# Two transformer blocks on one Trainium2 core: modulation chunks moved, convolution steps spread, two loops turned

## The chip, the cores and the metric

One of the eight cores of a Trainium2 chip runs the whole program. Its engines work side by side and each takes its own instructions in order: TensorE (PE; its weight loads are shown as PEld), VectorE (DVE), ScalarE (ACT), GpSimd (POOL) and SyncE (SP), which issues loads. They wait for one another by semaphores. The metric is the device time of one execution in microseconds (us), the median of several runs.

## The reference, cut to what matters

Two layers of a first block, then one layer of a second, on 256 tokens of width 1024, all in float32:

```python
for l in range(2):                                    # the first layers
    h = rms_norm(x, norm_mix_pre[l]); proj = h @ w_in[l]
    # a: compressed, selected and windowed attention; d: windowed attention with sinks
    # b: c = a * sigmoid(gate); causal depthwise convolution, 31 taps; layer_norm; silu
    # c: pooling over 2, 4, 8, 16 tokens, minus the input, times a matrix
    up = einsum("bsnc,ncd->bsnd", branches, w_branch[l])
    gates = sigmoid(h @ w_gate[l])
    mix = sum_n(gates * up) @ w_o[l]
    x = x + rms_norm(mix, norm_mix_post[l])
    hf = rms_norm(x, norm_ffn_pre[l])
    u = causal_depthwise_conv(hf @ ffn_w_up[l], ffn_conv_w[l], ffn_conv_b[l])
    f = (gelu(gate(u)) * val(u)) @ ffn_w_down[l]
    x = x + rms_norm(f, norm_ffn_post[l])
# second block: it is modulated by silu(c) @ w_mod + b_mod and silu(c_ctx) @ w_mod + b_mod (6 x 1024 values
# each), then state space scan, attention, mixture of experts
```

The modulation depends on `c` and `c_ctx` alone, not on `x`, so its product can be computed at any time before the second block.

## The kernel before, in words

**Chunks and the ring.** All weights stream from HBM in chunks of 1 MB (128 x 2048 floats) through a ring of four slots. A first layer has 92 chunks, so layer 1 starts in slot 0 again. Chunk c lies in slot c % 4. SP (`sync_program`, line 445, its load is line 450) takes the slots in turn: it waits until the slot's chunk is released (`used`), then issues the load of the chunk four places later, which reports to `landed`. PE releases a chunk with its last matmul (`done_with`) or, after `release`, with the first matmul of what it does next (`carry`).

**Split chunks.** Most products are made of three passes of a faster format. ACT copies a landed chunk to a rounded high part (`split_hi`, line 415, instruction at 423), DVE subtracts it from the chunk for the low part (`split_lo`, line 425, instruction at 428, written to `ring_low` at the same slot), and PE multiplies high by high, high by low and low by high. The high parts have buffers of their own, two up to the output product, so chunk n's high part waits until PE is through with chunk n - 2; in the FFN stage there are four. Both splits stand at fixed places in ACT's and DVE's programs. "Raw" chunks (modulation, compression) are multiplied as they land.

**Order of the chunks in a layer.** Input projections (kv, kv2, q, dq, two chunks each; 24 matmuls a chunk), c, ba, bg with the compression between, 16 gate chunks, 8 branch ("up") chunks, 4 of the output product `w_o` (wo), 22 of the FFN, 11 of down. Modulation: a layer computes half of its 6 x 1024 columns x 2 in 6 steps of 512 columns, each of two raw chunks, or halves (`mod_half`, line 487, matmuls at 495, four of them on 32 output rows each), copied by ACT (`mod_out`), summed and turned by PE (`mod_turn`, line 503, 508), and added up by DVE (`mod_in`). Before, halves stand behind gate chunks 2, 3, 5, 6, 8, 9 and FFN chunks 1, 3, 6, 8, 11, 13.

**Rounds.** Attention runs in six rounds beside the gate chunks, two gate chunks a round (PE's loop: `scores`, a gate chunk, `turn_probs`, a gate chunk, `values`). DVE's round r: `mask` of both halves (1299), the split of gate chunk 2r + 1, `out_low`, `weigh` (1326), the split of 2r + 2, 12 convolution steps (`conv_steps`, 1255; a step is one of 31 taps on one of 4 channel blocks, 124 in all, line 1267). In round 1 the weighing of the compressed attention (`cmp_weigh`, 1345) follows the split. PE transposes its result (`cpT`) behind gate chunk 2. Two more stretches of 8 and 6 steps follow the rounds.

**Branches.** PE makes 16 products `up`, four for each branch in the order pooling, a, d, b (`BRANCH_ORDER` = 2, 0, 3, 1). DVE multiplies each by its gate, POOL adds them up. Between them DVE does the steps that are left (3, 5, 3, 5, then all). PE transposes the finished convolution before product (0, 3) (`CONV_BEFORE`, `conv_turns`), DVE normalises it (`conv_norm`, POOL takes the root), PE transposes it back before (3, 1) and (3, 2) (`OB_BEFORE`), ACT applies silu, and DVE's low parts of it (`ob_lo`) are needed by branch b. 

**Output product and down.** Both go over column halves c outermost; for each of wo's chunks, or of down's, both token tiles t of 128 are multiplied. When (c, t) is complete ACT squares it (`post_square`, line 1083), and when both halves of a tile have squares, POOL takes the root, DVE adds the normalised tile to x (`residual`, 1467), ACT squares x (887), POOL takes the root, ACT (892) and DVE (1146) scale, and PE transposes the tile (`turn_normed`, 482). The order of the splits around it is written out, for ACT in these lines; DVE's (1472) are alike:

```python
for c in range(2):                                        # line 1085
    for n in range(FIRST_WO + 2 + 2 * c, FIRST_WO + 4 + 2 * c):
        split_hi(act, n)          # c = 0: wo 2, 3; c = 1: FFN 0, 1
    for t in range(TT):
        post_square("wo", c, t)
```

At the end of layer 0 ACT and DVE do the next layer's splits 0 and 1 (`heads`: `highs`, `lows`, lines 437 to 443, called at 1124 and 1510) ahead of the squares and the residual of down's c = 1. Between layer 1 and block 2 all engines meet at a barrier.

**PSUM regions.** `plan_layer` (line 215) fixes the region of every product; `claim` waits until the one before it in that region is drained.

Of the kernel before, what the change touches and what calls it, by code (L numbers as in the profile page):

```python
# [214 lines left out]
def plan_layer(jobs):  # L215
    for t in range(TT):
        for c in range(2):
            jobs.plan(("ht", t, c))
# [40 lines left out]
    for i in range(MOD_STEPS // 2):  # L259
# [18 lines left out]
    for i, r in zip(range(3, MOD_STEPS), ("s0", "s1", "t")):  # L278
# [7 lines left out]
CONV_BEFORE = (0, 3)  # L286
OB_BEFORE = {(3, 1): 0, (3, 2): 1}
# [3 lines left out]
def layer_block(nc, l, mem, ring, ring_low, landed, used, wts, psum, sems, cols_dram, rows_dram, turner_in, placed, wait_x, wait_scratch):  # L291
# [161 lines left out]
    def tensor_program(pe):  # L453
# [32 lines left out]

        def mod_half(i, half):
# [28 lines left out]
        def next_split():  # L516

            n = split_at["n"]
            split_at["n"] += 1
            assert state["chunk"] == SPLIT_CHUNKS[n], (state, n)  # L520
# [11 lines left out]
        pe.wait_ge(turner_in, 16)  # L532
        turn_normed("ht", 1)

        for w in ("kv", "kv2", "q", "dq"):
            for half in range(2):
# [19 lines left out]
                else:  # L556
                    jobs.fill(mm, (w, 1))
                    release(w)

# [242 lines left out]
        for c in range(2):  # L802
            for half in range(2):
                hi, lo = (part.rearrange("p (k n) -> p k n", k=4) for part in next_split())
                for i in range(2):
                    pe.wait_ge(mix_lo, 2 * half + i + 1)
                for t in range(TT):
                    name, ts = ("wo", c, t), slice(t * P, (t + 1) * P)
                    if half == 0:
                        jobs.claim(pe, name)  # L810
                    for k in range(4):
                        kk = 4 * half + k
                        mm = pe.matmul(jobs.out(name), mixS[:, 0, kk, ts], hi[:, k, :], start=(kk == 0), stop=False)
                        if k == 0:
                            carry(mm)
                        pe.matmul(jobs.out(name), mixS[:, 0, kk, ts], lo[:, k, :], start=False, stop=False)
                        mm = pe.matmul(jobs.out(name), mixS[:, 1, kk, ts], hi[:, k, :], start=False, stop=(kk == KD - 1))
                    if half == 1:
                        jobs.fill(mm, name)
                if half == 0:  # L820
                    done_with(mm)
                else:
                    release(("wo", c, 1))

        turn_normed("hf", 2)
# [20 lines left out]
        for i in range(FB // 2):  # L846
            hi, lo = (part.rearrange("p (q n) -> p q n", q=BLOCKS) for part in next_split())
            for t in range(TT):
                ts = slice(t * P, (t + 1) * P)
                for q in range(BLOCKS):  # L850
                    c, n = divmod(BLOCKS * i + q, FB)
                    name = ("down", c, t)
                    if n == 0:
                        jobs.claim(pe, name)
                    if c == 0 and t == 0:
                        pe.wait_ge(f_ready, n + 1)
# [2303 lines left out]
```

## Time and profile before

| | us |
|---|---|
| median of 3 runs (1822.49 to 1829.71) | 1823.33 |
| the profiled execution's own time | 1830.08 |
| its span, first to last instruction | 1828.0 |
| PE busy | 1680.5 |
| DVE busy | 1084.7 |
| ACT busy | 760.2 |
| POOL busy | 261.6 |

The mean granted clock of TensorE is 0.951 of 2.4 GHz. Layer 0 fills the span's first 548 us, layer 1 ends at about 1090, the rest is block 2. The span is 2 us shorter than the execution's own time. In a row of a profile L482 is line 482 of the kernel, `out<-in` are the program's names, and `<-` in brackets or behind a bar names who ended the idle time before an instruction.

### The profile page before, as it was taken

How to read it: one execution, taken by the hardware profiler on the slowest of the kernel's cores; microseconds unless marked ns; L12 is line 12 of the kernel's file. 1: busy time of each engine (PE TensorE's matmuls, PEld its weight loads, DVE VectorE, ACT ScalarE, POOL GpSimd, SP SyncE). 2: the span in 40 equal slices, each digit the busy share in tenths (PEclk: the TensorE clock that was granted, in tenths of full speed). 3: DMA queues.
4: the chain of work that ended last, by engine and by line, in shares of the span. 5: the costliest groups of instructions: out<-in, count | busy, mean ns of one | idle time of the engine just before them, and what ended most of it. 6: DMA issues, size and time to landing. Idle time of an engine off the chain costs nothing. (4 is left out here: it accounts for less than half of the span.)

```text
span 1828.0 us, 26603 instructions
## 1 busy us (share of the span) xinstructions
PE 1680.5 (92%) x10712; PEld 1383.9 (76%) x10712; DVE 1084.7 (59%) x1490; ACT 760.2 (42%) x1069; POOL 261.6 (14%) x293
## 2 busy tenths in 40 slices
PE   7998997899998989998899989999898978999996
PEld 5887897699977888887799974445475537899995
DVE  4668987566645668987566631284547334454555
ACT  4355654455534355554455422113116224333431
POOL 0200004144301200003144200014320000000000
PEclk9999998899999999998899999999869987999998
DMA  6544454466553545454466554112000232355551
GB/s 252 185 185 162 185 185 151 149 234 250 184 200 139 211 157 184 169 178 158 151 237 224 187 185 170 69 69 91 25 23 1 70 115 93 139 184 184 184 182 70
DMA packets 40121, 282.07 MB, mean 154 GB/s; under 512 B 4816, under 2 KB 5072, under 8 KB 6864
## 3 DMA queue, kind: packets, MB, share of 16 engines
q1 hardware_dynamic: 38432, 273.15, 41.4%
q10 hardware_dynamic: 1584, 7.42, 1.2%
q8 instruction: 78, 1.28, 0.3%
q14 instruction: 27, 0.22, 0.0%
HBM read 279.50 MB, written 1.05 MB: 153 GB/s over the span
## 5 line engine op out<-in xcount | busy, mean ns | idle before, releaser
L428 DVE TENSOR_TENSOR ring_low<-ring,sb_hi 128x2048 fp32r<-128x2048 f32 x116 | 267.9, 2309 | 192.3 <-ACT sb_hi L423 191.9
L423 ACT ACTIVATE sb_hi<-ring 128x2048 fp32r<-128x2048 f32 x116 | 222.5, 1918 | 285.9 <-DMA ring<-weights 114.4
L577 PE MATMUL psum<-sb_hS,sb_hi 128*128 128x256 f32 x704 | 203.3, 289 | 4.8 <-DVE ring_low L428 4.7
L1848 DVE TENSOR_TENSOR sb_split<-ring,sb_split 128x2048 fp32r<-128x2048 f32 x48 | 109.9, 2292 | 153.2 <-ACT sb_split L1843 153.2
L580 PE MATMUL psum<-sb_hS,sb_hi 128*128 128x256 f32 x704 | 200.3, 284 | 0.0
L581 PE MATMUL psum<-sb_hS,ring_low 128*128 128x256 f32 x704 | 199.4, 283 | 0.0
L839 PE MATMUL psum<-sb_hfT,ring_low 128*128 128x256 f32 x704 | 198.1, 281 | 0.0
L2162 PE MATMUL psum<-sb_hfS,sb_split 128*128 128x256 f32 x512 | 146.5, 286 | 6.0 <-DVE sb_hfS L2692 3.9
L2165 PE MATMUL psum<-sb_hfS,sb_split 128*128 128x256 f32 x512 | 145.8, 285 | 0.0
L2166 PE MATMUL psum<-sb_hfS,sb_split 128*128 128x256 f32 x512 | 145.8, 285 | 0.0
L577 PEld LDWEIGHTS psum<-sb_hS,sb_hi 128*128 128x128 f32 x704 | 134.9, 192 | 14.1 <-DVE ring_low L428 7.2
L581 PEld LDWEIGHTS psum<-sb_hS,ring_low 128*128 128x128 f32 x704 | 136.3, 194 | 0.0
L580 PEld LDWEIGHTS psum<-sb_hS,sb_hi 128*128 128x128 f32 x704 | 134.7, 191 | 0.0
L839 PEld LDWEIGHTS psum<-sb_hfT,ring_low 128*128 128x128 f32 x704 | 134.5, 191 | 0.0
L428 DVE TENSOR_TENSOR ring_low<-ring,sb_hi_ffn 128x2048 fp32r<-128x2048 f32 x34 | 79.7, 2350 | 64.2 <-ACT sb_hi_ffn L423 64.2
L1843 ACT ACTIVATE sb_split<-ring 128x2048 fp32r<-128x2048 f32 x48 | 91.4, 1906 | 54.2 <-PE psum L2130 18.1
L835 PE MATMUL psum<-sb_hfT,sb_hi_ffn 128*128 128x256 f32 x384 | 109.9, 286 | 1.3 <-DVE sb_hfT L1153 1.3
L838 PE MATMUL psum<-sb_hfT,sb_hi_ffn 128*128 128x256 f32 x384 | 109.7, 286 | 0.0
L2162 PEld LDWEIGHTS psum<-sb_hfS,sb_split 128*128 128x128 f32 x512 | 99.3, 194 | 8.3 <-issue 8.0
L1267 DVE SCALAR_TENSOR_TENSOR sb_acc<-sb_bglu,sb_cols,sb_acc 128x256 f32<-128x256 f32 x240 | 101.5, 495 | 0.0
L2165 PEld LDWEIGHTS psum<-sb_hfS,sb_split 128*128 128x128 f32 x512 | 99.3, 194 | 0.3
L2166 PEld LDWEIGHTS psum<-sb_hfS,sb_split 128*128 128x128 f32 x512 | 99.2, 194 | 0.0
(392 smaller groups left out, 3881.7 us busy)
## 6 DMA issues: line engine op xcount, KB each, us to landing
ring<-weights SPq DMA_DIRECT2D x256, 1024.0 KB, 4.8
sb_rows_ffn<-rows ACTq DMA_DIRECT2D x4, 512.0 KB, 4.7
sb_rows_mix<-rows ACTq DMA_DIRECT2D x2, 1024.0 KB, 5.0
sb_rows<-rows ACTq DMA_DIRECT2D x1, 2048.0 KB, 9.1
sb_x<-x_in SPq DMA_DIRECT2D x2, 512.0 KB, 5.9
sb_y<-ctx_in SPq DMA_DIRECT2D x1, 1024.0 KB, 6.4
out<-sb_x SPq DMA_DIRECT2D x2, 512.0 KB, 2.7
sb_const<-const SPq DMA_DIRECT2D x1, 711.0 KB, 13.5
```

Source lines behind the costliest of these rows:

```text
L423: act.activation(hi_of(n), ring[:, c % SLOTS, :], ACT.Copy).then_inc(hi_ready, 1)
L428: eng.tensor_tensor(low_of(n), ring[:, SPLIT_CHUNKS[n] % SLOTS, :], hi_of(n).bitcast(F32), ALU.subtract).then_inc(lo_dve, 1)
L577: mm = pe.matmul(out, hi[:, k, bs], hS[:, 0, k, :], start=(k == 0), stop=False)
L580: pe.matmul(out, hi[:, k, bs], hS[:, 1, k, :], start=False, stop=False)
L581: mm = pe.matmul(out, lo[:, k, bs], hS[:, 0, k, :], start=False, stop=(k == KD - 1))
L835: mm = pe.matmul(out, hi[:, k, b * P:(b + 1) * P], hfT[:, 0, k, :], start=(k == 0), stop=False)
L838: pe.matmul(out, hi[:, k, b * P:(b + 1) * P], hfT[:, 1, k, :], start=False, stop=False)
L839: mm = pe.matmul(out, lo[:, k, b * P:(b + 1) * P], hfT[:, 0, k, :], start=False, stop=(k == KD - 1))
L1848: dve.tensor_tensor(split[:, n % SPLITS, 1, :], ring[:, (first_moe + n) % SLOTS, :], split[:, n % SPLITS, 0, :].bitcast(F32), ALU.subtract ...
L2162: mm = pe.matmul(out, hi[:, k, b * P:(b + 1) * P], hfS[:, 0, k, :], start=(k == 0), stop=False)
L2165: pe.matmul(out, hi[:, k, b * P:(b + 1) * P], hfS[:, 1, k, :], start=False, stop=False)
L2166: mm = pe.matmul(out, lo[:, k, b * P:(b + 1) * P], hfS[:, 0, k, :], start=False, stop=(k == KD - 1))
```

## The change

Six halves a layer move. Two (step 0) now stand between the two chunks of kv, and PE does them at the layer's head: in layer 1 before it transposes the normalised tiles, in layer 0 behind. Four (steps 3 and 4) stand between wo's last chunk and the FFN's first. The other six are behind gate chunks 2, 3, 6, 7 and FFN chunks 11, 13. PSUM regions, `mod_out`, `mod_turn` and `mod_in` follow them. Convolution steps are given per round, 102 in place of 84; all that are left come behind the first product; its transposes move from product (0, 3) to (2, 3), those of the branch from (3, 1), (3, 2) to (0, 2), (3, 0). `cmp_weigh` goes ahead of a split. The last two chunks of wo and of down are multiplied tile by tile: both chunks for t = 0, then both for t = 1. No matmul is added or removed; the placing of the splits around wo's squares and of the next layer's first splits is not changed. The diff, cut:

```diff
-MOD_AFTER_GATE = {2: (0, 0), 3: (0, 1), 5: (1, 0), 6: (1, 1), 8: (2, 0), 9: (2, 1)}
-TURN_AFTER_GATE = {4: 0, 7: 1, 10: 2}
-MOD_AFTER_FFN = {1: (3, 0), 3: (3, 1), 6: (4, 0), 8: (4, 1), 11: (5, 0), 13: (5, 1)}
-TURN_AFTER_FFN = {5: 3, 10: 4, 15: 5}
+HEAD_MODS = [(0, 0), (0, 1)]
+MOD_AFTER_GATE = {2: (1, 0), 3: (1, 1), 6: (2, 0), 7: (2, 1)}
+TURN_AFTER_GATE = {4: 1, 8: 2}
+MODS_AFTER_WO = [(3, 0), (3, 1), (4, 0), (4, 1)]
+MOD_AFTER_FFN = {11: (5, 0), 13: (5, 1)}
+MOD_OUT_IN_FFN = {1: 3, 3: 4, 14: 5}
+TURN_AFTER_FFN = {3: 3, 7: 4, 15: 5}
...
-    return ["split"] * FIRST_BA + ["raw", "split"] * 4 + gates + ["split"] * 12 + ffn + ["split"] * (FB // 2)
+    return (["split"] + ["raw"] * len(HEAD_MODS) + ["split"] * (FIRST_BA - 1) + ["raw", "split"] * 4 + gates + ["split"] * 12
+            + ["raw"] * len(MODS_AFTER_WO) + ffn + ["split"] * (FB // 2))
...
-CONV_BEFORE = (0, 3)
-OB_BEFORE = {(3, 1): 0, (3, 2): 1}
+CONV_BEFORE = (2, 3)
+OB_BEFORE = {(0, 2): 0, (3, 0): 1}
+CONV_STEPS = (4, 20, 16, 14, 16, 14, 18)
...
+        def head_mods():
+            if wait_down is not None:
+                wait_down(pe)
+            for i, half in HEAD_MODS:
+                state["chunk"] = 1 + half
+                mod_half(i, half)
+            state["chunk"] = 0
...
         pe.wait_ge(turner_in, 16)
+        if l > 0:
+            head_mods()
         turn_normed("ht", 1)
+        if l == 0:
+            head_mods()
...
+            if w == "kv":
+                mod_turn(0)
...
+        last = []
+        for t in range(TT):
             for half in range(2):
...
+                if t == 0:
+                    last.append([part.rearrange("p (k n) -> p k n", k=4) for part in next_split()])
+                mm = mix_product(1, half, t, *last[half])
+                if (t, half) == (1, 0):
+                    mm.then_inc(used[(state["chunk"] - 2) % SLOTS], 1)
+        release(("wo", 1, 1))
+
+        for i, half in MODS_AFTER_WO:
+            mod_half(i, half)
         turn_normed("hf", 2)
...
-        for n in range(FIRST_UP + 2, FIRST_UP + 6):
+        for n in range(FIRST_UP + 2, FIRST_UP + 4):
             split_hi(act, n)
         for t in range(TT):
-            if t == 1:
-                split_hi(act, FIRST_UP + 6)
+            split_hi(act, FIRST_UP + 4 + t)
             jobs.wait_filled(act, ("obT", t))
...
+            if r == 1:
+                cmp_weigh()
             split_lo(dve, FIRST_GATE + 2 * r + 1)
...
-            if r == 1:
-                cmp_weigh()
...
-            conv_steps(12)
+            conv_steps(CONV_STEPS[r])
...
                 if i % 2 == 0:
-                    conv_steps(3)
+                    conv_steps(4 * TAPS)
                 else:
                     chunk = 2 * bi + i // 2
...
                     if chunk < 7:
                         split_lo(dve, FIRST_UP + chunk + 2)
-                    conv_steps(5 if chunk < 2 else 4 * TAPS)
...
+        conv_roots()
         k = 0
         for n in BRANCH_ORDER[1:]:
...
-                if (n, i + 1) == CONV_BEFORE:
-                    conv_roots()
...
+    kv0 = k_split(kv[:, 0:512])
     chunks = [
-        k_split(kv[:, 0:512]), k_split(np.concatenate([kv[:, 512:768], w[:, 1816:2072]], 1)),
+        kv0[0:1], *[mod[j][half] for j, half in HEAD_MODS], kv0[1:2], k_split(np.concatenate([kv[:, 512:768], w[:, 1816:2072]], 1)),
...
-        k_split(i["w_o"][l][:, 0:512]), k_split(i["w_o"][l][:, 512:1024]), *ffn,
+        k_split(i["w_o"][l][:, 0:512]), k_split(i["w_o"][l][:, 512:1024]),
+        *[mod[j][half] for j, half in MODS_AFTER_WO], *ffn,
```

Down's last two chunks are turned like wo's.

## Rows read from the trace of the kernel before

**Rows 1.** The page: PE's busy time and the granted clock in 40 slices.

```profile
PE 1680.5 (92%) x10712; PEld 1383.9 (76%) x10712; DVE 1084.7 (59%) x1490; ACT 760.2 (42%) x1069; POOL 261.6 (14%) x293
...
PEclk9999998899999999998899999999869987999998
```

**Rows 2.** Waits of PE up to 556 us: us in total, times, longest.

```profile
PE psum L482 <- ACT sb_tm L892: 25.6, 3, 11.4
...
PE psum L482 <- DVE sb_acc L1267: 8.2, 1, 8.2
...
PE psum L794 <- issue: 1.3, 1, 1.3
```

**Rows 3.** Groups of PE, whole run: modulation halves and turns; busy us, mean ns.

```profile
L495 PE MATMUL psum<-ring,sb_cvec 128*32 128x512 f32 x192 | 25.6, 605 | 0.0
...
L508 PE MATMUL psum<-sb_const,sb_mrow 128*128 128x2 f32 x96 | 11.4, 240 | 0.0
```

**Rows 4.** Stretches: us, busy PE, PEld, DVE, ACT, POOL, clock, DMA share, GB/s.

```profile
8.30:18.20 9.90, 5.72 (x21) 4.99 (x22) 6.88 (x8) 7.86 (x9) 2.30 (x4) 1.00 1.01 424
...
286.70:293.90 7.20, 7.20 (x52) 7.20 (x51) 4.24 (x8) 2.63 (x2) 3.05 (x6) 0.80 0.18 49
...
344.20:354.40 10.20, 7.25 (x33) 6.88 (x34) 5.25 (x7) 4.24 (x7) 2.25 (x3) 0.50 0.58 206
```

**Rows 5.** DVE in time order, rounds 0 and 1: start us, us, what.

```profile
134.16 3.25 DVE L1267 SCALAR_TENSOR_TENSOR sb_acc<-sb_bglu,sb_cols,sb_acc 128x256 f32<-128x256 f32 x8
...
139.96 2.28 DVE L428 TENSOR_TENSOR ring_low<-ring,sb_hi 128x2048 fp32r<-128x2048 f32 x1
...
149.50 4.83 DVE L1267 SCALAR_TENSOR_TENSOR sb_acc<-sb_bglu,sb_cols,sb_acc 128x256 f32<-128x256 f32 x12
```

**Rows 6.** The same kind of stretch, DVE alone, rounds 2 to 5: busy us.

```profile
158.04:221.35 63.31, 57.81 (x94) 1.00 0.53 196
```

**Rows 7.** PE in time order, single rows where the stages begin.

```profile
29.14 0.40 PE L547 MATMUL psum<-sb_hi,sb_hS 128*128 128x512 f32 x1
...
144.34 0.48 PE L482 MATMUL psum<-sb_const,sb_csc 128*128 128x128 f32 x1 [6.03 <-DVE sb_csc L1357]
...
221.41 0.39 PE L577 MATMUL psum<-sb_hS,sb_hi 128*128 128x256 f32 x1 [0.32 <-DVE ring_low L428]
...
346.50 0.47 PE L482 MATMUL psum<-sb_const,sb_tm 128*128 128x128 f32 x1 [6.62 <-ACT sb_tm L892]
...
555.48 0.45 PE L482 MATMUL psum<-sb_const,sb_tm 128*128 128x128 f32 x1 [7.54 <-ACT sb_tm L892]
```

**Rows 8.** ACT in time order around the output product of layer 0.

```profile
329.06 1.92 ACT L423 ACTIVATE sb_hi<-ring 128x2048 fp32r<-128x2048 f32 x1 [5.10 <-PE psum L813]
...
332.01 3.97 ACT L423 ACTIVATE sb_hi_ffn<-ring 128x2048 fp32r<-128x2048 f32 x2
...
337.15 0.60 ACT L1083 ACTIVATE sb_acc<-psum 128x512 f32<-128x512 f32 x1 [1.17 <-PE psum L817]
...
339.92 0.60 ACT L1083 ACTIVATE sb_acc<-psum 128x512 f32<-128x512 f32 x1 [2.08 <-PE psum L817]
```

**Rows 9.** DVE in time order, the same stretch.

```profile
331.01 2.29 DVE L428 TENSOR_TENSOR ring_low<-ring,sb_hi 128x2048 fp32r<-128x2048 f32 x1 [4.66 <-ACT sb_hi L423]
...
340.00 1.28 DVE L1467 SCALAR_TENSOR_TENSOR sb_x<-sb_tm,sb_small,sb_x 128x1024 f32<-128x1024 f32 x1 [0.50 <-POOL sb_small L1533]
```

**Rows 10.** SP in time order: the load of gate chunk 4.

```profile
138.48 0.33 SPq L450 DMA_DIRECT2D ring<-weights  x1
```

**Rows 11.** Loads of the ring issued from 316 to 335 us (four).

```profile
DMA to landing us min/median/max: 4.8/4.8/4.9
```

**Rows 12.** ACT and DVE in time order at the end of layer 0.

```profile
543.82 1.92 ACT L423 ACTIVATE sb_hi<-ring 128x2048 fp32r<-128x2048 f32 x1 [0.98 <-DMA ring<-weights]
...
547.98 0.60 ACT L1083 ACTIVATE sb_acc<-psum 128x512 f32<-128x512 f32 x1 [1.66 <-PE psum L861]
...
549.16 1.28 DVE L1467 SCALAR_TENSOR_TENSOR sb_x<-sb_tm,sb_small,sb_x 128x1024 f32<-128x1024 f32 x1 [0.50 <-POOL sb_small L1533]
```

More of the change, by code:

```diff
@@ L258, in plan_layer @@
             jobs.plan(("O", a, t), "u", drains=2)
-    for i in range(MOD_STEPS // 2):
+    for i in range(1, MOD_STEPS // 2):
         jobs.plan(("mod", i), "t")
@@ L277, in plan_layer @@
         jobs.plan(("ffn", j))
-    for i, r in zip(range(3, MOD_STEPS), ("s0", "s1", "t")):
+    for i, r in zip(range(3, MOD_STEPS), ("s0", "t", "s1")):
         jobs.plan(("mod", i), r)
@@ L800, in tensor_program, with mix_product @@
                 release(name)
-        for c in range(2):
-            for half in range(2):
[L804 to L823, printed above, removed]
+        def mix_product(c, half, t, hi, lo):
+            name, ts = ("wo", c, t), slice(t * P, (t + 1) * P)
+            if half == 0:
+                jobs.claim(pe, name)
+            for k in range(4):
+                kk = 4 * half + k
+                mm = pe.matmul(jobs.out(name), mixS[:, 0, kk, ts], hi[:, k, :], start=(kk == 0), stop=False)
+                if k == 0:
+                    carry(mm)
+                pe.matmul(jobs.out(name), mixS[:, 0, kk, ts], lo[:, k, :], start=False, stop=False)
+                mm = pe.matmul(jobs.out(name), mixS[:, 1, kk, ts], hi[:, k, :], start=False, stop=(kk == KD - 1))
+            if half == 1:
+                jobs.fill(mm, name)
+            return mm
@@ new lines, in tensor_program @@
+        for half in range(2):
+            hi, lo = (part.rearrange("p (k n) -> p k n", k=4) for part in next_split())
+            for i in range(2):
+                pe.wait_ge(mix_lo, 2 * half + i + 1)
+            for t in range(TT):
+                mm = mix_product(0, half, t, hi, lo)
+            if half == 0:
+                done_with(mm)
+            else:
+                release(("wo", 0, 1))
+        last = []
+        for t in range(TT):
+            for half in range(2):
+                if t == 0:
[3 more added lines that the diff above has]
+                    mm.then_inc(used[(state["chunk"] - 2) % SLOTS], 1)
@@ L847, in tensor_program @@
+        for i in range(FB // 2 - 2):
             hi, lo = (part.rearrange("p (q n) -> p q n", q=BLOCKS) for part in next_split())
             for t in range(TT):
[L849 to L856, printed above, removed]
[L857 to L863 removed]
@@ L864, in tensor_program @@
-            if i < FB // 2 - 1 and n < FB - 1:
+                mm, n = down_product(i, t, hi, lo)
+            if n < FB - 1:
                 done_with(mm)
             else:
-                release(name)
+                release(("down", 0, 1))
+        last = []
+        for t in range(TT):
+            for i in range(2):
+                if t == 0:
+                    last.append([part.rearrange("p (q n) -> p q n", q=BLOCKS) for part in next_split()])
+                mm, n = down_product(FB // 2 - 2 + i, t, *last[i])
+                if (t, i) == (1, 0):
+                    mm.then_inc(used[(state["chunk"] - 2) % SLOTS], 1)
@@ L868, in tensor_program @@
+        release(("down", 1, 1))
         jobs.wait_filled(pe, ("down", 1, 1))
```

59 lines of the change are left out of this document (39 added, 20 removed).

## The prediction

> **What bounds the kernel now.** I read the page first: the first two sections. TensorE (PE) is busy for 92% of the span, at a granted clock of 0.951 on average, that is 2.4 GHz nearly everywhere [rows 1]. So nothing that merely moves PE's work gains anything; only PE's idle stretches, and the stretches at the lower clock level behind them, can be won. Second, PE's waits. Up to 556 us (all of layer 0 and the head of layer 1) the three waits for the normalised tile come to 25.6 us, of which 11.4 is the start of the run; the convolution holds PE for 8.2 us, the branch parts for 1.3 [rows 2], the compressed weights for 6.03 [rows 7]. Layer 1 repeats them to within 0.2 us. The change aims at all of these. Third, the granted clock behind a wait: 0.50 from 344.2 to 354.4 us, 0.80 over 286.7 to 293.9 [rows 4]. The latter is 20% of 7.2 us = 1.4 us lost, and some 1 us more in the transposes ahead of it, 2.4 in all. Last, the order of instructions on ScalarE (ACT) and VectorE (DVE) around each idle stretch, which decides this case.
>
> **Modulation halves.** A half is 25.6 us / 24 = 1.07 us busy [rows 3], some 1.0 us of displacement as its end overlaps the next matmul. A turn is 11.4 / 12 = 0.95 us. Moving them is worth at most that: a layer has 12 halves, 6 of them now in the FFN stage, of which 4 leave: -4.0 us there. The other cost is where their chunks stand in the ring of 4 slots. A load is issued only when the chunk four places earlier is released, and it lands 4.8 us later [rows 11]. Splitting it takes 1.9 us on ACT and 2.3 on DVE [rows 8, 9]. Backlogged loads come faster: 424 GB/s at the start [rows 4], 2.5 us per 1 MB chunk. I use 4.8 us after the issue or 2.5 us after the landing before, whichever is later.
>
> **Head of a layer.** The order is now kv0, two halves, kv1, kv2. The load of kv2's first chunk waits for kv0's release, so it is ready for PE 4.8 + 0.2 + 1.9 + 2.4 = 9.3 us later; PE has only kv1 (24 matmuls, 5.6 us, twice the 2.8 us between the two squares [rows 8]) and a turn of 0.95. It waits 2.8 to 2.9 us. In layer 0 the halves add some 1.3 us before kv0's release, since one wait of 1.1 us hides part. So kv2, which began at 29.14 [rows 7], begins 1.3 + 0.95 + 2.9 = **5.2 us later**.
>
> In layer 1 the halves lie in the gap before 555.48. But the splits of the next layer's first two chunks are issued by ACT and DVE ahead of the squares and the residual of down's second half. The second split is ring chunk 3 now, not 1, and its slot is that of down's very last chunk, released when down is complete. Before, it began at 543.82, and the last square, which marks down's end, at 547.98 [rows 12]. After: the load is issued 0.2 us behind that, landed 553.0, split by ACT 555.0, squares only then, DVE's low part until 557.3, post_gain 0.7, the residual of tile 0 from 557.95 instead of 549.16 [rows 12]: **8.8 us later**, and PE's transposes with it (they follow its end by 5.0 us, before and after). Then the same kv2 delay, 0.95 + 2.9 or 3.0. Together 12.7.
>
> **Rounds.** Convolution steps take 4.83 / 12 = 0.40 us [rows 5]. Round 0 has 4 instead of 12 and the weighing precedes a split. DVE's order then: the first 4 steps end at 134.16, mask 2.7 (from the end of the next 8 steps, 137.3, to the split at 139.96), weigh the compressed part 2.1 (from the split's end, 142.2, to 144.3, when PE's wait of 6.03 ends [rows 7]), split 2.3, so that wait shrinks to below 1 and gate chunk 3 starts 5 us earlier. But then DVE runs late: it weighs round 1 (143.4), waits for the high part of gate chunk 4 (issued at 138.48 [rows 10], landed at 143.3 in either kernel, 1.9 on ACT), splits until 147.5, and does 20 steps, until 155.5. Round 2's mask begins at 155.5, 2.5 us before the old 158.04, and some 4 us after its scores are there. From 158.04 to 221.35 DVE was busy 57.8 of 63.3 us [rows 6]. 10 more steps in rounds 2 to 4 are 4.0 us, against 5.5 idle, of which an estimated 4 (waits for scores and for a load) can go. So that stretch lasts about 63 us again, and gate chunk 11, at 221.41 [rows 7], starts **2.5 us earlier**, though two halves and a turn (3 us) have left the rounds before it: DVE has become the bound. Bounds: 0, if ACT's exps slip too, and 6.5, if DVE had room. I take 2.5, since the row of busy time is the nearer. The cover that is used up is DVE's slack: 86% busy before.
>
> **Convolution.** 116 steps are done before the branch products instead of 98. The last 8 (3.2 us) end after the first product, PE's transposes three products in then find them done. The wait of 8.24, the 1.29 for the branch parts and 2.4 of lower clock go. What is late next is the split of up chunk 3: ACT may start it only when chunk 1's buffer is free, DVE does conv_norm (3.6 us) first: 1.0 us. **10.9 earlier**. GpSimd's roots go ahead of its additions, and wait for nothing that those need.
>
> **Output product, tile outermost.** Its last chunk is needed 2.8 us earlier, but its high part shares a buffer with the second one and starts only at 329.06, released by PE [rows 8]; the low part ends at 333.30 [rows 9]. PE wants it at 331.3: 2.0 us of wait. Tile 0 is complete 0.9 us earlier, tile 1 and the stage 2.0 later. Down has four buffers, its last chunk is split long before; no cost, and no gain as tile 1 still comes last and the barrier follows.
>
> **The gap before the FFN.** This is the largest term. ACT issues the splits of FFN chunks 0 and 1 between the squares of the two column halves: the 3.97 us at 332.01, then the squares at 337.15 and 339.92 [rows 8]. DVE likewise, ahead of the residual. With four halves in between, FFN chunk 0 has the slot of half 0, and half 0 is read only after the output product ends. Step by step on the clock of before: product ends 341.8; half 2 lands 344.1 (its slot is freed at 339.2), half 3 at 347.5, FFN chunk 0 at 350.0, chunk 1 at 352.5. ACT splits until 354.4, the squares start there and not at 337.15; the low part of chunk 1 ends at 356.7; the residual of tile 0 runs 357.4 to 358.7 (before: 340.00 to 341.28, [rows 9]), and the transposes follow 5.2 us later as they did: 363.9 against 346.50 [rows 7], **17.4 us later**, the 2.0 included. The four halves (4.0) are hidden there. The lower clock (10.2 us at 0.50 around 346.5 [rows 4]) is not saved: PE is idle for 15 us.
>
> The DMA page of the Trainium skill (DMA: Bandwidth & Descriptors, Bandwidth) puts HBM at some 358 GB/s per core. By it chunks would land 2.9 us apart, and each of these gaps would be 1 to 2 us longer, the total 3 us more. The measured 424 GB/s decides here.
>
> **Sum.** Layer 0: 5.2 - 2.5 - 10.9 + 17.4 - 4.0 = +5.2. Layer 1: 12.7 - 2.5 - 10.9 + 17.4 - 4.0 = +12.7. Block 2 is untouched. Total +17.9: span 1828.0 to 1845.9. The profiled execution took 1830.08, 6.8 above the median of 1823.33 and 0.4 above the slowest run; against the median this is **1841**.
>
> **Rivals.** *Chunks arrive in time, faster.* If the FFN chunks and kv1 were there before the squares, nothing would hold them: transposes would follow half 3, 2.0 us later than before, at the head 0. Layer 0: 5.2 - 2.5 - 10.9 + 2.0 - 4.0 = -10.2; layer 1: 3.9 - 2.5 - 10.9 + 2.0 - 4.0 = -11.5; 1801.6. It takes delays of squares (15.4 + 15.4 + 8.8 = 39.6) below some 22 to be not slower. For: loads overlap, and some of the lower clock would be won too. Against: four slots and in-order engines leave no way. *Rounds have slack.* DVE keeps up and the 6.5 us of the cpT wait come through: 8 less, 1833; the idle 5.5 of 63.3 us speak against it. *Rounds stall.* Each round gets later and ACT's exps and splits add to it: gate chunk 11 no earlier, and 2 us more in the up stage: 1850. *Little moves (within 0.5%).* Slot releases and splits overlap better by half (delays 8, 8, 4 instead of 15.4, 15.4, 8.8): 1822. *The change doesn't do what it says* for the last two down chunks: their order buys nothing, 0 us, within all cases.
>
> **Chances.** Forecast 0.58 (own range 1834 to 1850). Rounds with slack 0.09, rounds stalling 0.10, little moves 0.14, faster 0.09. A measurement of this kernel tells about 0.5% (9 us) from no change. Slower by more than that: 0.58 + 0.09 + 0.10 = 0.77, same 0.14, faster 0.09. The range of 8 in 10 goes from 1823, the upper part of the little-moves case, to 1855, stalled rounds with some longer stretches of the lower clock on top.
>
> **What would show it.** After the output product, ACT's idle before the split of FFN chunk 0, ended by the DMA, and squares 12 us or more behind PE's last matmul. PE's wait ahead of the FFN transposes near 15 us instead of 6.62, at layer 1's head near 13 instead of 7.54. A wait of some 3 us for the low part of kv2, of 2 for the last output chunk. No wait for the convolution. Waits of PE for low parts in the rounds, 1 to 3 us in each of rounds 2, 3 and 5. Squares that come at once behind the product would make all of it wrong; so would loads that land while the product still runs.

## The result and the profile after

The changed kernel takes 1855.18 us (median of 4, 1848.67 to 1857.83) against 1826.52 us of the kernel before: ratio 1.0151, 95% interval 1.0112 to 1.0191. Slower, as forecast, but at the far end: 1841 was the value, 1834 to 1850 its own range, and the median lies 0.2 us past the wide range (1823 to 1855). Run again beside 11 executions of the kernel before: 1852.27 against 1828.60 us, 1.0140 (1.0119 to 1.0161). The loss is 24 to 29 us.

The profiled execution, the quickest of its four, took 1848.67 us with a span of 1846.7 us. That is 18.7 us above the profiled span of before (1828.0), where 17.9 was forecast. The difference to the 24 to 29 us is spread: the profiled execution of before (1830.08) was near the upper end of that kernel's executions (1818.7 to 1831.0 in 61 of them), the one of after at the lower end of its own.

The page of the changed kernel [rows 1]:

```profile
PE 1676.5 (91%) x10712; PEld 1375.5 (74%) x10712; DVE 1084.4 (59%) x1490; ACT 760.3 (41%) x1069; POOL 243.7 (13%) x293
```

PE does the same work in 4 us less, and the span is longer: everything lost is idle time. Waits of PE up to 566 us (shortly before the end of layer 1's head gap), changed kernel [rows 2]; us in total, times, longest:

```profile
PE psum L489 <- ACT sb_tm L945: 25.9, 2, 14.5
PE psum L601 <- DVE ring_low L435: 10.1, 6, 2.6
PE psum L511 <- DMA ring<-weights: 4.1, 3, 2.7
PE psum L833 <- DVE ring_low L435: 2.8, 2, 1.8
PE psum L524 <- ACT sb_mrow L954: 1.9, 1, 1.9
```

The 8.2 us for the convolution are gone, and of the 6.0 for the compressed weights 0.7 are left. The 25.9 us for the normalised tile are two waits, not three, the third (13.22 us) ends at 568.12, outside this stretch. New are waits for the low parts of gate chunks in the rounds (L601, 10.1 us against 2.4 before), for the halves' loads, for the last output chunk, for the copy of the modulation row.

Layer 0 by stage, as five stretches that begin with PE's instruction: the head's transposes, the transpose of the compressed part (rounds), the branch products, the output product, the FFN's transposes (to the next layer's). Columns as in [rows 4]. Kernel before:

```profile
11.40:144.30 132.90, 122.14 (x862) 105.99 (x862) 83.89 (x123) 62.83 (x96) 11.05 (x17) 0.99 0.53 195
144.30:256.80 112.50, 111.18 (x879) 97.25 (x879) 95.06 (x159) 66.10 (x118) 0.00 (x0) 0.98 0.49 178
256.80:316.20 59.40, 49.80 (x400) 49.22 (x401) 48.37 (x65) 22.82 (x22) 16.80 (x14) 0.91 0.45 160
316.20:346.50 30.30, 22.70 (x96) 17.89 (x96) 20.89 (x17) 16.63 (x20) 9.23 (x12) 0.96 0.40 139
346.50:555.50 209.00, 200.80 (x1409) 182.90 (x1409) 123.50 (x137) 101.27 (x120) 64.43 (x77) 0.97 0.58 210
```

Changed kernel, and behind the five the two stretches of low clock around the long gaps:

```profile
11.30:143.00 131.70, 124.75 (x887) 106.99 (x887) 78.81 (x115) 63.17 (x97) 11.05 (x17) 0.99 0.55 205
143.00:260.10 117.10, 107.75 (x855) 94.84 (x855) 106.99 (x185) 66.21 (x118) 0.00 (x0) 0.99 0.44 162
260.10:308.10 48.00, 47.46 (x400) 47.05 (x400) 40.72 (x47) 22.93 (x22) 14.67 (x14) 1.00 0.54 198
308.10:356.50 48.40, 27.90 (x129) 18.61 (x129) 21.09 (x17) 16.48 (x20) 10.16 (x12) 0.82 0.45 174
356.50:568.10 211.60, 196.20 (x1392) 180.51 (x1392) 124.39 (x137) 101.03 (x120) 56.15 (x77) 0.97 0.52 188
338.90:359.40 20.50, 4.84 (x22) 3.10 (x23) 12.34 (x11) 9.66 (x14) 7.72 (x10) 0.50 0.53 201
557.40:571.10 13.70, 2.98 (x14) 2.98 (x15) 10.12 (x10) 6.99 (x13) 7.75 (x10) 0.50 0.00 0
```

The branch stage falls from 59.4 to 48.0 us and has PE busy 47.5 of it: the gain that was meant. The output product with what follows it grows from 30.3 to 48.4 with 5.2 us more of work (the 4 halves). The rounds grow by 4.6 us although PE has 3.4 us less to do; DVE's work there rises from 95 to 107 us. PE's rows where it waits in the rounds, the last of them at gate chunk 11:

```profile
165.45 0.58 PE L601 MATMUL psum<-sb_hS,sb_hi 128*128 128x256 f32 x1 [2.60 <-DVE ring_low L435]
...
204.24 0.39 PE L601 MATMUL psum<-sb_hS,sb_hi 128*128 128x256 f32 x1 [2.30 <-DVE ring_low L435]
...
224.71 0.39 PE L601 MATMUL psum<-sb_hS,sb_hi 128*128 128x256 f32 x1 [2.26 <-DVE ring_low L435]
```

The order of events at the long gap in layer 0 [rows 7, 8, 9]: single rows of PE, then ACT, DVE.

```profile
325.27 0.50 PE L833 MATMUL psum<-sb_hi,sb_mixS 128*128 128x512 f32 x1 [1.79 <-DVE ring_low L435]
...
333.53 0.40 PE L837 MATMUL psum<-sb_hi,sb_mixS 128*128 128x512 f32 x1
...
340.02 1.93 PE L511 MATMUL psum<-ring,sb_cvec 128*32 128x512 f32 x8 [2.72 <-DMA ring<-weights]
356.50 0.90 PE L489 MATMUL psum<-sb_const,sb_tm 128*128 128x128 f32 x3 [14.54 <-ACT sb_tm L945]
...
342.47 1.91 ACT L430 ACTIVATE sb_hi_ffn<-ring 128x2048 fp32r<-128x2048 f32 x1 [18.44 <-DMA ring<-weights]
344.94 1.91 ACT L430 ACTIVATE sb_hi_ffn<-ring 128x2048 fp32r<-128x2048 f32 x1 [0.57 <-DMA ring<-weights]
346.76 0.58 ACT L1137 ACTIVATE sb_acc<-psum 128x512 f32<-128x512 f32 x1
...
350.27 1.28 DVE L1521 SCALAR_TENSOR_TENSOR sb_x<-sb_tm,sb_small,sb_x 128x1024 f32<-128x1024 f32 x1 [0.49 <-POOL sb_small L1587]
```

The product ends at 333.9. ACT is idle for 18.44 us in front of the split of FFN chunk 0, ended by the DMA, and the first square starts 12.9 us behind the product's end, behind two such splits. It is the square of tile 0, which in the turned order was complete at about 328.3, 5.6 us ahead of the product's end. PE, with the halves done at 341.95, waits 14.54 us. At layer 1's head ACT does the same for kv's second chunk:

```profile
556.57 1.91 ACT L430 ACTIVATE sb_hi<-ring 128x2048 fp32r<-128x2048 f32 x1 [11.90 <-DMA ring<-weights]
558.38 0.58 ACT L1137 ACTIVATE sb_acc<-psum 128x512 f32<-128x512 f32 x1
```

### The profile page after: what moved, and what is told of

It is laid out like the page before. It is cut to its first block and busy times, and to the rows that moved or that the text cites. A ratio compares the mean times of both kernels' runs of the same rounds, so it can differ in the third digit from the quotient of the medians.

```text
span 1846.7 us, 26597 instructions
## 1 busy us (share of the span) xinstructions
PE 1676.5 (91%) x10712; PEld 1375.5 (74%) x10712; DVE 1084.4 (59%) x1490; ACT 760.3 (41%) x1069; POOL 243.7 (13%) x293
## 5 line engine op out<-in xcount | busy, mean ns | idle before, releaser
L601 PE MATMUL psum<-sb_hS,sb_hi 128*128 128x256 f32 x704 | 203.7, 289 | 20.2 <-DVE ring_low L435 20.1
L601 PEld LDWEIGHTS psum<-sb_hS,sb_hi 128*128 128x128 f32 x704 | 135.1, 192 | 30.9 <-DVE ring_low L435 24.0
L1896 ACT ACTIVATE sb_split<-ring 128x2048 fp32r<-128x2048 f32 x48 | 91.4, 1906 | 54.2 <-PE psum L2183 18.1
L430 ACT ACTIVATE sb_hi_ffn<-ring 128x2048 fp32r<-128x2048 f32 x34 | 65.2, 1918 | 82.4 <-DMA ring<-weights 75.2
```

The lines of the kernel that those rows point to most:

```text
L430: act.activation(hi_of(n), ring[:, c % SLOTS, :], ACT.Copy).then_inc(hi_ready, 1)
L601: mm = pe.matmul(out, hi[:, k, bs], hS[:, 0, k, :], start=(k == 0), stop=False)
```

## The experiments

Theory: three things that the change carries along cost what it loses, namely splits that wait for late chunks ahead of the squares (FFN chunks 0 and 1; kv's second chunk), and convolution steps ahead of the gate chunks' low parts. Rivals: the halves themselves, the turned orders, the clock. Each median stands against the kernel before in the same session (1827.6 to 1828.9 us), 11 to 18 executions of it. Medians of different sessions are compared directly below; the kernel before differed by 1.3 us between them.

**1. The convolution part alone, on the kernel before.**

```diff
-CONV_BEFORE = (0, 3)
-OB_BEFORE = {(3, 1): 0, (3, 2): 1}
+CONV_BEFORE = (2, 3)
+OB_BEFORE = {(0, 2): 0, (3, 0): 1}
+CONV_STEPS = (4, 20, 16, 14, 16, 14, 18)
...
-            conv_steps(12)
+            conv_steps(CONV_STEPS[r])
...
```

> The kernel before with the convolution part of the change alone (steps spread over the rounds, its normalisation and transposes moved to the third branch, ACT's and DVE's splits of the up chunks placed accordingly); no half and no chunk order is touched. Theory (the loss is all in the halves' new places, the convolution part is a pure gain): the wait of 11 us for the convolution goes, wo starts 10 to 13 us earlier in each layer, the time is 20 to 26 us below the kernel before, about 1803 us. Rival (the spread steps make VectorE the bound of the rounds, and it is the halves that left the rounds that pay for it): the gates stage gets 3 to 6 us longer in each layer and the gain is 10 to 14 us, about 1814 us.

1809.50 us, ratio 0.9900 (0.9878 to 0.9923), 19 us below the kernel before. Between theory and rival: its rounds and its branch stage are

```profile
138.40:257.20 118.80, 111.83 (x879) 97.36 (x879) 107.14 (x186) 66.37 (x119) 0.00 (x0) 0.97 0.49 178
...
257.20:305.20 48.00, 47.48 (x400) 47.08 (x400) 40.73 (x47) 22.93 (x22) 14.69 (x14) 1.00 0.55 198
```

So the branch stage gives 11.4 us a layer and the head some 6 (the wait of 6.03), and the rounds take 6.3 of it back: 118.8 against 112.5 us with the same work of PE. This part alone beats both kernels. The rounds grew as the rival said, and here no half has left them.

**2. The same, with the steps distributed otherwise.**

```diff
-CONV_STEPS = (4, 20, 16, 14, 16, 14, 18)
+CONV_STEPS = (4, 13, 18, 14, 11, 18, 22)
```

> The convolution part alone with other numbers of steps in the rounds (4, 13, 18, 14, 11, 18, 22 instead of 4, 20, 16, 14, 16, 14, 18). Theory (in the changed rounds VectorE's steps stand ahead of the low parts of the gate chunks, 0.4 us each, and these are what TensorE waits for): the waits of 2.7 and 2.0 us in rounds 2 and 5 go, 3 to 4.5 us less in each layer, about 1802 us. Rival (the waits come from ACT's splits or from the DMA and only move): within 2 us of the run with 20 and 16, about 1809 us.

1795.54 us, ratio 0.9824 (0.9804 to 0.9844): 14 us less than with the first distribution, more than the 7 expected. Rounds of layer 0, and PE's waits in the rounds, first of this kernel:

```profile
137.30:250.10 112.80, 109.75 (x879) 94.95 (x879) 106.23 (x184) 65.80 (x119) 0.00 (x0) 1.00 0.51 187
```

```profile
PE psum L578 <- DVE ring_low L429: 2.2, 3, 0.9
```

and of the one with 20 and 16 steps:

```profile
PE psum L578 <- DVE ring_low L429: 5.6, 3, 2.7
```

With the smaller waits of the stretch 7.7 us of waiting have become 3.7. 4.0 us of waits have gone and 6.0 us of time: the granted clock of the stretch is 1.00 instead of 0.97, and PE's busy time for the same 879 matmuls falls by 2.1 us. These 2.1 us belong to one of the two long waits: behind the wait of 2.75 us (it ends at 161.01) the clock was 0.72 over 10 us, behind the one of 1.98 us (221.82) it was 1.00. DVE's rounds hold 100 steps instead of 102; the two others are done behind the first branch product, where the stage grows from 48.0 to 49.6 us. Both layers' rounds together give 11.8 of the 14 us.

**3. FFN chunks 0 and 1 split behind the normalisation.**

```diff
 for c in range(2):
-    for n in range(FIRST_WO + 2 + 2 * c, FIRST_WO + 4 + 2 * c):
-        split_hi(act, n)
+    if c == 0:
+        for n in range(FIRST_WO + 2, FIRST_WO + 4):
+            split_hi(act, n)
     for t in range(TT):
         post_square("wo", c, t)
 squares_of(1)
 norm_first(1)
+for n in range(FIRST_FFN, FIRST_FFN + 2):
+    split_hi(act, n)
```

(DVE's low parts alike, behind `norm_second`.)

> The changed kernel, with the splits of FFN chunks 0 and 1 (ACT's and DVE's) moved from ahead of the squares of the output product's second half to behind the normalisation's last instruction on each engine. Theory (these splits wait for chunks whose slots are freed late, and the squares stand behind them): the squares start right behind the product, 10 to 12 us earlier, the wait of 14.5 us ahead of the FFN's transposes falls to 2 to 5 us in both layers, the time falls by 18 to 24 us to about 1834 us. Rival (the halves on TensorE themselves, and not the splits, set the start of the FFN): the transposes can't start before the halves end, the gain is under 6 us in all, about 1850 us.

1835.85 us, ratio 1.0051 (1.0031 to 1.0071): 16 to 19 us below the changed kernel, at the lower edge of the 18 to 24 expected. ACT and PE at the gap (the trace is of an execution of 1843.86 us, the slowest of seven):

```profile
339.46 0.60 ACT L1137 ACTIVATE sb_acc<-psum 128x512 f32<-128x512 f32 x1 [5.26 <-PE psum L837]
...
347.83 1.91 ACT L430 ACTIVATE sb_hi_ffn<-ring 128x2048 fp32r<-128x2048 f32 x1 [2.70 <-DMA ring<-weights]
...
347.23 3.68 PE L489 MATMUL psum<-sb_const,sb_tm 128*128 128x128 f32 x16
...
356.78 0.55 PE L874 MATMUL psum<-sb_hfT,sb_hi_ffn 128*128 128x256 f32 x1 [5.87 <-DVE sb_hfT L1210]
```

The squares are now released by PE's product and nothing else; the transposes follow the halves with no wait. A new wait of 5.87 us stands behind them: the late splits now delay the high and low parts of the normalised tile. The cost of such a split moves with it, wherever something urgent stands behind it.

**4. The halves between product and FFN put back.**

```diff
-MODS_AFTER_WO = [(3, 0), (3, 1), (4, 0), (4, 1)]
-MOD_AFTER_FFN = {11: (5, 0), 13: (5, 1)}
+MODS_AFTER_WO = []
+MOD_AFTER_FFN = {1: (3, 0), 3: (3, 1), 6: (4, 0), 8: (4, 1), 11: (5, 0), 13: (5, 1)}
...
```

> The changed kernel with the four halves between the output product and the FFN put back among the FFN's blocks, where they stood before (head, rounds, convolution and tile orders stay changed). Theory: FFN chunks 0 and 1 land some 10 us earlier again and the wait ahead of the FFN's transposes is 6 to 8 us as in the kernel before; 20 to 22 us between product and transposes become 7, the FFN gets 6 us longer, 8 to 10 us gained in each layer, about 1837 us. Rival (the turned tile order of the output product is what delays the FFN's chunks, since it frees the slots later): the wait stays over 10 us and the gain is under 6 us in all, about 1850 us.

1830.51 us, ratio 1.0016 (1.0001 to 1.0030): 22 to 25 us less, more than the 18 expected. The FFN chunks' splits run inside the product again, and PE's wait is

```profile
326.07 3.85 ACT L430 ACTIVATE sb_hi_ffn<-ring 128x2048 fp32r<-128x2048 f32 x2
...
343.35 0.90 PE L489 MATMUL psum<-sb_const,sb_tm 128*128 128x128 f32 x3 [5.76 <-ACT sb_tm L945]
```

The turned order is still in this kernel, so it is not what delays the chunks. This is the largest single loss of the change.

**5. kv's second chunk ahead of the halves in the ring.**

```diff
-                state["chunk"] = 1 + half
+                state["chunk"] = 2 + half
...
-        kv0[0:1], *[mod[j][half] for j, half in HEAD_MODS], kv0[1:2], k_split(np.concatenate([kv[:, 512:768], w[:, 1816:2072]], 1)),
+        kv0[0:1], kv0[1:2], *[mod[j][half] for j, half in HEAD_MODS], k_split(np.concatenate([kv[:, 512:768], w[:, 1816:2072]], 1)),
```

> The changed kernel with the first two halves put behind kv's second chunk in the order of the ring (chunks 2 and 3 instead of 1 and 2), so that kv's second chunk no longer waits for the slot of the last down chunk; TensorE's order is unchanged. Theory: at the second layer's head the squares no longer stand behind that split, the wait ahead of the transposes falls from 13.2 to 4 to 6 us, the time falls by 7 to 10 us to about 1846 us; the first layer's head stays. Rival (the squares wait for something else, the drains of the down product or the two halves on TensorE): under 2 us, about 1854 us.

1846.80 us, ratio 1.0112 (1.0090 to 1.0133): 5.5 to 8.4 us less, where 7 to 10 were expected. The split is out of the way of the second square, which PE releases; the first, of tile 0, still stands behind it:

```profile
552.99 1.92 ACT L430 ACTIVATE sb_hi<-ring 128x2048 fp32r<-128x2048 f32 x1 [2.62 <-DMA ring<-weights]
554.81 0.58 ACT L1137 ACTIVATE sb_acc<-psum 128x512 f32<-128x512 f32 x1
...
557.26 0.60 ACT L1137 ACTIVATE sb_acc<-psum 128x512 f32<-128x512 f32 x1 [1.78 <-PE psum L899]
```

PE's wait ahead of the transposes is gone, where 4 to 6 us were expected to stay; in its place PE waits 2.33 and 1.11 us for the loads of the two halves and begins the transposes right behind them, at 564.56. From the FFN's transposes of layer 0 to those of layer 1's head the trace has 202.3 us instead of 211.6, 9.3 less. But layer 0's head got 6.9 us longer (138.6 against 131.7; below, run 9), so the gain in time is what is left of the two.

**6. Both repairs (4 and 5) together.**

> The changed kernel with both repairs: the four halves back among the FFN's blocks, and the first two halves behind kv's second chunk in the ring. Theory (the two losses are at different places and add): the changed kernel's 1853 us less 24 and less 8, about 1822 us; this is 10 us above the run that has the same convolution part and the same turned orders but no half moved (1811.7 us), and these 10 us stand in the two heads and the rounds (TensorE's wait of 2 us for the turned rows' copy, kv2's chunks a place later, three waits instead of two in the rounds, each with a stretch of half clock behind it). Rival (one repair makes the other void, or the chunks collide again): over 1828 us.

1823.84 us (13 executions, 1820.27 to 1835.55), ratio 0.9984 (0.9969 to 0.9998). They add up: 29.5 us less than the changed kernel (1853.3), where the two alone gave 22.8 and 6.5.

**7. The turned orders alone, on the convolution part.** Both loops over the last two chunks as in the changed kernel, no half moved.

> The kernel before with the convolution part and the turned tile orders of the output and down products (no half is moved). Theory (a turned order finishes token tile 0 some 2.8 us sooner ahead of the end of the product, but TensorE waits 1.8 us for the product's last split): the wait of 6.5 us ahead of the FFN's transposes becomes 4 us and one of about 2 us stands in the product; 1 us or less a place, the time within 3 us of the run with the convolution part alone, about 1808 us. Rival (the turned order is a gain that the halves' damage hid): 2.5 us at each of four places, about 1800 us. Second rival (the first of the last chunks is freed late and costs more than that): about 1813 us.

1811.65 us, ratio 0.9915 (0.9894 to 0.9935), 2 us above run 1 and not to be told from it. In its trace the FFN's wait is 5.76 us instead of 6.52, and a wait of 1.8 us for the last split stands in the product: the stage takes 31.5 us against 30.4, in layer 1 33.1 against 30.3. The turn gains nothing.

**8. The output product's order put back in the changed kernel.**

```diff
-        for t in range(TT):
-            for half in range(2):
...
-                mm = mix_product(1, half, t, *last[half])
...
+        for half in range(2):
...
+            for t in range(TT):
+                mm = mix_product(1, half, t, hi, lo)
...
```

> The changed kernel with the output product's last two chunks in their old order (both token tiles of a chunk, then the next chunk). Theory (the halves' chunks and the splits behind them set the start of the FFN, not this order): TensorE's wait of 1.8 us for the last split goes, the halves' chunks have their slot freed 3 us sooner; 1 to 4 us less a layer, about 1850 us. Rival (the turned order is what lets the squares start early, and it is lost): 2 to 3 us more a layer, about 1860 us.

1848.06 us, ratio 1.0111 (1.0091 to 1.0131), 4 us less than the changed kernel in the same session (1852.27). The wait of 1.8 us goes, and the stage takes 46.4 us instead of 48.3; the gap stays, since the DMA sets it:

```profile
339.02 1.06 PE L511 MATMUL psum<-ring,sb_cvec 128*32 128x512 f32 x8 [3.37 <-DMA ring<-weights]
355.52 0.69 PE L489 MATMUL psum<-sb_const,sb_tm 128*128 128x128 f32 x2 [15.43 <-ACT sb_tm L944]
```

**9. Both repairs, old orders, the steps of run 2.** It differs from run 2 only by the two halves in each head and the places of the others in the rounds.

> The changed kernel with both repairs, both tile orders back and the other numbers of steps (4, 13, 18, 14, 11, 18, 22), so that it differs from the run with these numbers and no half moved (1795.5 us) only by two halves in each head and by the places of the four in the rounds. Theory (a half in TensorE's gap at the head is cheap in itself, but kv2's chunks come later and TensorE waits for the turn's row, some 3 us a head with the clock behind it; in the rounds two halves less are worth as much as their 1.5 us each): 4 to 8 us above it, about 1801 us. Rival (halves in the gaps are the gain they are meant to be once nothing stands behind them): 3 to 6 us below it, about 1791 us.

1813.92 us, ratio 0.9922 (0.9904 to 0.9939): 18 us above run 2, where 4 to 8 were expected; the sign was right, the size wrong. Layer 0's head and rounds:

```profile
11.70:150.50 138.80, 128.94 (x887) 108.38 (x887) 78.72 (x115) 63.07 (x97) 11.03 (x17) 0.99 0.51 194
...
150.50:262.60 112.10, 106.91 (x855) 93.66 (x855) 106.28 (x183) 65.91 (x118) 0.00 (x0) 1.00 0.46 170
```

and the head of run 2:

```profile
11.60:137.30 125.70, 120.28 (x863) 104.75 (x863) 78.66 (x114) 62.61 (x96) 11.04 (x17) 1.00 0.52 197
```

In the rounds the two halves that left give 0.7 us for 2.8 us of work; in the head they cost 13.1 (layer 1: 7.7, from the starts of the stages, 133.4 against 125.7). PE's rows say why:

```profile
18.60 1.94 PE L511 MATMUL psum<-ring,sb_cvec 128*32 128x512 f32 x8 [0.56 <-DMA ring<-weights]
...
35.62 1.02 PE L524 MATMUL psum<-sb_const,sb_mrow 128*128 128x2 f32 x8 [2.07 <-ACT sb_mrow L944]
37.45 0.50 PE L569 MATMUL psum<-sb_hi,sb_hS 128*128 128x512 f32 x1 [0.80 <-DVE ring_low L435]
```

A half takes 1.94 us here and not 1.07, as PE runs at half its pace this early (kv's matmuls too, until 24 us; run 2 was at full pace from 16.4, which makes some 3.6 of the 13.1 us); then come the turn (1.02), 2.07 us for the copy of the row and 0.80 for kv2, 3.9 us together. kv2 starts 9.8 us later; the other 3.3 us come behind it, where the granted clock is 0.80 up to 46 us and PE waits another 1.08 us for a low part. In run 2 kv2 starts at about 27.6 (its matmuls run on without a wait from 16.37, 48 of them), here at 37.45. In layer 0 there is no gap to put a half in. In layer 1 there is one, and the stage with the gap takes as long as in run 2 (207.3 against 207.2 us); what is lost there is lost behind it, where PE waits 1.97 us for the copy of the row and 0.62 for kv2 and then has 0.58 of the clock for 7 us.

**10. The changed kernel with the steps of run 2.** `CONV_STEPS` as in run 2, no other edit.

> The changed kernel with the other numbers of steps in the rounds (4, 13, 18, 14, 11, 18, 22) as its one edit. Theory (two of the three waits of TensorE in its rounds come from the steps standing ahead of the gate chunks' low parts, whatever became of the halves, and a stretch of half clock follows each): the rounds get 4 to 6 us shorter in each layer, 8 to 14 us in all, about 1842 us. Rival (with two halves fewer in the rounds the waits come from elsewhere): under 4 us, about 1850 us.

1850.24 us, ratio 1.0138 (1.0113 to 1.0163): 2 to 5 us less than the changed kernel by the medians and nothing by the ratios (1.0140 there), where 8 to 14 were expected. The rounds did what was expected; here they are, then the output stage and the FFN of layer 0,

```profile
145.90:257.70 111.80, 106.73 (x855) 93.66 (x855) 106.24 (x183) 65.98 (x118) 0.00 (x0) 1.00 0.47 170
306.60:356.40 49.80, 28.53 (x129) 19.68 (x129) 21.03 (x17) 16.49 (x20) 10.20 (x12) 0.82 0.44 170
356.40:570.30 213.90, 198.74 (x1392) 182.89 (x1392) 124.73 (x137) 101.21 (x120) 58.15 (x77) 0.95 0.52 185
```

and the same of the changed kernel run again:

```profile
145.50:261.50 116.00, 106.63 (x854) 93.58 (x854) 107.01 (x185) 66.27 (x118) 0.00 (x0) 1.00 0.46 164
309.50:357.80 48.30, 27.91 (x129) 18.62 (x129) 21.08 (x17) 16.48 (x20) 10.18 (x12) 0.82 0.47 175
357.80:569.40 211.60, 196.24 (x1392) 180.56 (x1392) 124.55 (x137) 101.08 (x120) 56.45 (x77) 0.97 0.53 187
```

4.2 us are won in the rounds (6.5 in layer 1), all of it waits: PE is busy for the same 106.7 us at a clock of 1.00 in both, though one of the waits that went was of 2.74 us. And 3.8 are given back in these two stages behind: PE is busy 2.5 us longer in the FFN for the same 1392 matmuls, at 0.95 of the clock instead of 0.97. Why the clock came back later there is not shown; the gap ahead is the same length (16.5 us from the start of the fourth half to the transposes in both).

**11. The changed kernel again.**

> The changed kernel again, to have its time and the granted clock of its executions beside many of the kernel before on one chip. Theory (the profiled execution of the changed kernel, 1848.7 us, was a quick one of its spread, and the one of before, 1830.1 us, a slow one): median 1853 to 1857 us against 1828 to 1829 us, and executions that differ by some 8 us do so by their mean granted clock (0.943 against 0.947) and not by a wait. Rival (the quick and the slow executions differ in a DMA's landing): the same clock, other waits.

1852.27 us (1850.11 to 1856.49), ratio as given at the top. The median is 0.7 us below the range expected. The quickest execution has the highest mean granted clock (0.946 at 1850.11) and the slowest the lowest (0.943 at 1856.49), but in between the order isn't kept: 1852.27 has 0.943 and 1853.32 has 0.945. Their waits are not known, as only the profiled one left a trace; that the clock is the cause, and not a companion, is not shown.

## Why the prediction was right, and where it was off

Medians of neighbouring kernels make a chain: before 1828.9; convolution part 1809.5 (-19.4); turned orders 1811.7 (+2.2); two halves in the heads, four in other places of the rounds 1823.8 (+12.2); these halves ahead of kv's second chunk 1830.5 (+6.7); four halves behind the output product 1853.3 (+22.8, the median of all nine executions of the changed kernel). The end is 24.4 above the start, and each step is known to some 2 to 3 us. By the forecast's terms:

- **The gap before the FFN**, 17.4 less 4.0 a layer, 26.8 in all. Measured 22.8 + 2.2 = 25.0. In the trace the transposes start at 356.50, 10.0 us later than before, where 9.2 was forecast, behind a wait of 14.54 (forecast "near 15"); the stage from the output product to them grew by 18.1 us, in layer 1 by 19.5 (forecast 17.4); squares 12.9 us behind the product (forecast "12 us or more"), ACT's idle ended by the DMA, 1.79 us for the last output chunk (forecast 2.0). Right in mechanism and size. The loads of the FFN chunks came at the backlog's pace as assumed: the two splits ended by the DMA start 2.47 us apart, 1 MB each, 425 GB/s. The Trainium skill (DMA: Bandwidth & Descriptors, Bandwidth) gives some 358 GB/s for a core when both cores of a memory domain stream, which would be an estimated 2.9 us a chunk, and 425 GB/s for 16 MB measured on one core with the pair's other core idle. This program runs on one core, and the trace agrees with the second figure; the prediction named only the first.
- **Layer 1's head**, 8.8 us for the split of kv's second chunk. In the trace the gap from down's last matmul to the transposes grew from 7.54 to 16.6 us, by 9.1; two pairs of medians give 6.7 and 5.5 to 8.4, net of what the other order costs in layer 0's head. PE's wait 13.22 (forecast "near 13"), ACT's split at 556.57 (forecast 553.0 on the clock of before, 558.2 with layer 0's 5.2 ahead of it).
- **The convolution**, 10.9 a layer. The branch stage fell by 11.4, the output product began 8.1 us earlier (forecast 8.2). Right.
- **The rounds** are the step that failed: -2.5 was taken from the start of kv2 to gate chunk 11, with bounds of 0 and -6.5 and a rival of stalled rounds at 0.10. Layer 0 gave +0.5 (kv2 +2.8, gate chunk 11 at 224.71 against 221.41 [rows 7]) and layer 1 +3.0 (kv2 +16.3, gate chunk 11 +19.3, where 15.4 was forecast). The forecast saw that DVE becomes the bound and named PE's waits for low parts, 1 to 3 us each (measured 2.60, 2.30 and 2.26 at L601), but its sum has no term for them: it set the 4.0 us of added steps against DVE's idle time, whatever low part stands behind them, and it had nothing for a clock that falls behind such a wait. Run 1 shows the miss with no half moved: 19.4 us gained where the two terms for rounds and convolution come to 26.8. Run 2 shows the cause: 13 steps instead of 20 in round 1 and 11 instead of 16 in round 4, and 14 us are won (with 18, 18 and 22 in rounds 2, 5 and 6 for 16, 14 and 18).
- **The halves at the head** were costed at 1.3 + 0.95 + 2.9 in layer 0 and hold in the profiled execution (+2.8 instead of +5.2 at kv2, since PE happened to be at full pace at 16.69, and in the trace of before only at 20.05; +3.7 in layer 1 for 3.9); against the kernel without them they cost more: 12.2 us by the chain, with the rounds, against 5.2 + 3.9 = 9.1 in the two heads. The forecast's single wait of 2.8 to 2.9 us for kv2 came as two, 1.86 for the copy of the row (L524) and 0.80 for kv2, 2.66 together. What it did not have is the clock behind them: 0.73 from 31.9 to 38 us, and 0.81 from 586.5 to 600 us in layer 1.
- **The FFN stage**, -4.0: in layer 1 it took 200.2 us instead of 206.7 (-6.5), in layer 0, up to down's last matmul, 195.0 instead of 201.4 (-6.4). PE was busy 6.7 us less, of which four halves at 1.07 us are 4.3; its mean clock was 0.99 instead of 0.98. Block 2, forecast as untouched, took 2.0 us less in the profiled pair; no run shows why.

The sum was right in the profiled pair (18.7 for 17.9) partly by luck: the rounds were 8.5 us too low and the gap before the FFN 2.8, and against them stand 4.9 in the FFN stages, 2.6 at kv2, 2.0 in block 2 and 1.2 in the branch stages. Against all executions it was 6.5 short: heads, rounds and convolution were forecast at 9.1 - 5.0 - 21.8 = -17.7 and gave -19.4 + 12.2 = -7.2; the other terms were 3.9 too high. A further 5.5 us of the miss are the reference point: three executions of before had a median of 1823.33, eighteen had 1828.85. The rival of stalling rounds took place in part: gate chunk 11 came no earlier, as it says, and the 2 us more in the up stage did not come; its chance (0.10) was too low. "Chunks arrive in time" fell with the trace of the changed kernel, where ACT's splits wait 18.44 and 11.90 us for the DMA, and run 4 shows what in-time chunks are worth.

## What to carry to other kernels

With a ring of slots and engines that work in order, an instruction that needs a chunk may stand only behind everything that is more urgent than that chunk, or the chunk must be surely there: before a load is put into the stream, follow the four chunks behind it to their slots, and see what stands behind their splits. Filling a gap of TensorE with other work is worth nothing if its loads push back the work that ends the gap. Work spread over a vector engine is to be spread by what stands behind it in that engine's program (here the low parts that TensorE needs next), and not by counts alone: the same 124 steps cost or gave 14 us by their places.

## What the runs showed of the hardware

- A short wait of PE in full work was often, not always, followed by a stretch at half the clock. Over the 13 traces, waits of PE for low parts of gate chunks of 2.5 to 2.8 us had a granted clock below 0.95 in the 4 us behind them in 17 of 21 cases, those of 1.8 to 2.5 us in 17 of 47, those of 1.0 to 1.8 us in none of 9. The same wait in the same place went both ways: 2.75 us in run 1 with 0.50 behind it, 2.74 us in run 11 with 1.00. Run 2 won 6.0 us for 4.0 us of waits removed, run 10 4.2 us for its waits alone. Waits of 14.54 and 13.22 us had 20.5 and 13.7 us at 0.50 around them, mostly idle.
- At the start of the run PE's pace differed between executions with a granted clock of 1.00 in the rows: the first kv matmuls took 0.80 and 0.63 us each in run 9 until about 24 us, and 0.50 and 0.40 from the first in the changed kernel. 0.63 us is what such a matmul takes at half the clock elsewhere (0.50 from 587 to 590.4 us in the changed kernel), so up to about 24 us the clock shown does not tell PE's pace. Runs 5 and 6 have the same first head, and PE reaches the modulation turn at 35.35 and at 32.65 us: 2.7 us that no edit made.
- A load that stood alone landed 4.8 us after its issue, backlogged ones followed 2.47 us apart.
